# A two-layer transformer on one core: rows turned four tiles at a time, stores of the gating between weight loads, semaphores cleared by GpSimd

## The reference

```python
# layer 0 (layer 1 has another attention and no gating)
sh_a, sc_a, g_a, sh_m, sc_m, g_m = split(silu(c) @ w_mod[l] + b_mod[l])   # and the same for c_ctx
h  = x   * (1 + sc_a)  + sh_a          # "modulated" rows, the input of every projection
hc = ctx * (1 + csc_a) + csh_a
# mixer_ab: window attention on 512 columns, gating on the other 512
u, gv = gelu(h @ w_in[:, 768:1280]), gelu(h @ w_in[:, 1280:])
vn    = layer_norm(gv)                                  # (chunks of 128 tokens, 8 groups, 64)
b_out = u * (einsum('gpq,bnqgc->bnpgc', w_s, vn) + b_s)
y     = concat([a_out, b_out], -1) @ w_out              # and the same for ctx
x     = layer_norm(ALPHA * x + g_a * y)
x     = layer_norm(ALPHA * x + g_m * (relu(modulate(x) @ w1) ** 2 @ w2))
```

## Time and profile before

| | us |
|---|---|
| median of three executions | 2984.6 |
| the profiled execution | 2985.59 |
| its span, first to last instruction | 2983.8 |
| modulation stage | 0 to 29.4 |
| rows stage (0, kind 0) | 29.4 to 61.7 |
| window stage | 61.7 to 461.6 |
| gating stage | 461.6 to 506.6 |
| block 0 | 506.6 to 1537.1 |
| second rows stage | 1537.1 to 1589.4 |
| attention stage | 1589.4 to 2147.5 |
| block 1 | 2147.5 to 2983.8 |

### The profile page before, as it was taken

One profiled execution on the slowest core, in us unless ns is written; L12 is line 12 of the kernel. 1 busy time (PEld: TensorE's weight loads), 2 busy tenths in 40 slices (PEclk: granted clock), 3 DMA queues, 4 the chain that ended last, 5 costly groups with the idle time before them and its releaser, 6 DMA issues. The chain is left out here.

```text
span 2983.8 us, 40578 instructions
## 1 busy us (share of the span) xinstructions
PE 2799.8 (94%) x15614; PEld 2296.1 (77%) x15614; DVE 1361.5 (46%) x2159; ACT 912.1 (31%) x1704; POOL 533.6 (18%) x365
## 2 busy tenths in 40 slices
PE   6999995999999999999957999999799999999998
PEld 3666774788888888888846888888677888888886
DVE  3575454563333333333383555555555333333336
ACT  4244553341121121111224344443433212211222
POOL 0000000341121121121140000000034223323321
PEclk7999997999999999999978999999999999999999
DMA  6574225441011010010042111110256111111112
GB/s 251 184 307 157 70 67 186 147 136 43 28 48 36 28 56 28 28 56 28 30 146 83 36 36 51 36 36 8 85 141 191 48 45 48 56 42 42 56 42 57
DMA packets 192673, 238.95 MB, mean 80 GB/s; under 512 B 15992, under 2 KB 153840, under 8 KB 186416
## 3 DMA queue, kind: packets, MB, share of 16 engines
q1 hardware_dynamic: 192272, 237.30, 24.8%
q10 hardware_dynamic: 288, 0.10, 0.0%
HBM read 203.72 MB, written 37.88 MB: 81 GB/s over the span
## 5 line engine op out<-in xcount | busy, mean ns | idle before, releaser
L2173 DVE TENSOR_TENSOR y<-y,pair 128x1024 f32<-128x1024 f32 x280 | 341.5, 1220 | 334.9 <-PE pair L2307 334.9
L2305 PE MATMUL pair<-m_wbh,m_ath 128*128 128x512 f32 x1120 | 437.1, 390 | 4.2 <-DVE y L2173 2.9
L2307 PE MATMUL pair<-m_wbh,m_atl 128*128 128x512 f32 x1120 | 437.9, 391 | 0.0
L2306 PE MATMUL pair<-m_wbl,m_ath 128*128 128x512 f32 x1120 | 436.9, 390 | 0.0
L2227 DVE TENSOR_TENSOR m_atl<-m_sq,m_ath 128x512 fp32r<-128x512 f32 x156 | 100.8, 648 | 646.2 <-POOL m_sq L2078 646.2
L2032 ACT ACTIVATE m_rel<-pair 128x512 f32<-128x512 f32 x160 | 88.9, 555 | 983.6 <-PE pair L2331 973.1
L2078 POOL TENSOR_TENSOR m_sq<-m_rel 128x512 f32<-128x512 f32 x160 | 155.2, 970 | 1125.6 <-ACT m_rel L2032 1125.5
L2331 PE MATMUL pair<-hth,m0n_wal 128*128 128x512 f32 (+1 forms) x768 | 272.2, 354 | 0.0
L2330 PE MATMUL pair<-htl,m0n_wah 128*128 128x512 f32 (+1 forms) x768 | 272.1, 354 | 0.0
L2329 PE MATMUL pair<-hth,m0n_wah 128*128 128x512 f32 (+1 forms) x768 | 271.5, 354 | 0.0
L2305 PEld LDWEIGHTS pair<-m_wbh,m_ath 128*128 128x128 f32 x1120 | 210.3, 188 | 50.3 <-DVE y L2173 4.6
(11 more groups left out here) (270 smaller groups left out, 5239.8 us busy)
## 6 DMA issues: line engine op xcount, KB each, us to landing
a_ring<-in_w_mod SPq DMA_DIRECT2D x40, 1024.0 KB, 9.1
m_rawb<-in_mlp_w SPq DMA_DIRECT2D x64, 512.0 KB, 4.4
m_rawa<-in_mlp_w SPq DMA_DIRECT2D x60, 512.0 KB, 4.1
x_rows<-r_res SPq DMA_DIRECT2D x28, 512.0 KB, 5.0
r_raw<-cat_cols SPq DMA_DIRECT2D x18, 512.0 KB, 6.3
mod_w<-in_w_mod SPq DMA_DIRECT2D x8, 1024.0 KB, 12.3
r_xin<-in_x SPq DMA_DIRECT2D x16, 512.0 KB, 4.3
gate_pre<-a0g_gout SPq DMA_DIRECT2D x20, 256.0 KB, 2.0
```

The source lines that it names most:

```text
L2173: dve.tensor_tensor(k.y[:, t, :], k.y[:, t, :], k.pair[t % 2][:, :], ALU.add).then_inc(s_y, 1)
L2305: pe.matmul(o, ath[:, m, ts], bh[:, m, cols], start=m == 0, stop=False)
L2306: pe.matmul(o, ath[:, m, ts], bl[:, m, cols], start=False, stop=False)
L2307: i = pe.matmul(o, atl[:, m, ts], bh[:, m, cols], start=False, stop=m == M - 1)
```

## The change

It has three parts.

The first replaces `stage_rows(0, 0)` by a new `stage_first`. All ten row tiles are loaded ahead by the modulation stage, each with a semaphore of its own. The tokens are taken in groups of 512, 512 and 256. In a group TensorE turns block kt of all its tiles next to each other into bank kt, so that one ScalarE instruction applies scale and shift to 512 (or 256) columns. There are 24 such steps of one kt and one group. The copy to `hth` is made by VectorE in the even steps and by ScalarE in the odd ones; VectorE subtracts in all. `modt` has four places.

The second part is in the gating: the loads of `ab_w_out` are issued one behind each of the first eight stores, and `bot` has six places, so that `leave(t)` waits for the store of tile t-6.

The third part hands `clear_last` to GpSimd in every stage (at the attention and the window stage behind GpSimd's first memsets).

```diff
@@ Kept
-    def clear_last(self, dve):
+    def clear_last(self, pool):
         for s in self.dead:
-            dve.sem_clear(s)
+            pool.sem_clear(s)
@@ stage_modulation
-    x_ahead = nc.alloc_sbuf_tensor_at("r00_xin", [P, 3, D], F32, offset=k.after_ht)
-    s_ahead = [k.early(f"r00_x{i}") for i in range(3)]
+    x_ahead = nc.alloc_sbuf_tensor_at("r00_xin", [P, XT + CT, D], F32, offset=k.after_ht)
+    s_ahead = [k.early(f"r00_x{t}") for t in range(XT + CT)]
...
-            for t in range(3):
-                sp.dma_start(x_ahead[:, t, :], io["x"][0][t * P:(t + 1) * P, :]).then_inc(s_ahead[t], 16)
+            for t in range(XT + CT):
+                x = (io["x"][0] if t < XT else io["ctx"][0])[t % XT * P:(t % XT + 1) * P, :]
+                sp.dma_start(x_ahead[:, t, :], x).then_inc(s_ahead[t], 16)
@@ new
+def stage_first(nc, io, k):
+    sb = Place(nc, "r00", k.after_ht)
+    xin, s_x = k.ahead["x"]
+    sb.at += (XT + CT) * D * 4
+    NB = 4
+    modt = sb("modt", [P, NB, 512])
+    assert sb.at <= k.window_head
+    head = Place(nc, "a0h", k.window_head)
+    ahead = {}
+    for x in "kv":
+        ahead[x] = head(f"raw{x}", [P, KT, P]), k.early(f"a0_raw_{x}")
+        head.at += 2 * KT * P * 4
+    k.ahead["kv"] = ahead
+    sem = lambda n: k.sem(f"r00_{n}")
+    s_tr, s_mod, s_ha, s_hd, s_hl = [sem(x) for x in ("tr", "mod", "ha", "hd", "hl")]
+    groups = groups_of(TOK)
+    steps = [(a, n, kt) for a, n in groups for kt in range(KT)]
+    by_act = lambda i: i % 2 == 1
+    with nc.Block() as block:
+        @block.sync
+        def _(sp):
+            for i, x in enumerate("kv"):
+                sp.dma_start(ahead[x][0][:, :, :], io["ab_w_in"][0].rearrange("(k p) n -> p k n", p=P)[:, :, 512 + i * P:512 + (i + 1) * P]).then_inc(ahead[x][1], 16)
+        @block.gpsimd
+        def _(pool):
+            k.clear_last(pool)
+        @block.scalar
+        def _(act):
+            def high(i):
+                a, n, kt = steps[i]
+                act.wait_ge(s_mod, i + 1)
+                act.activation(k.hth[:, kt, a:a + n], modt[:, i % NB, 0:n], ACT.Copy).then_inc(s_ha, 1)
+            for i, (a, n, kt) in enumerate(steps):
+                col = lambda part: k.mod[:, 0, part * KT + kt, a // SEQ:a // SEQ + 1]
+                act.wait_ge(s_tr, i + 1)
+                if i >= NB:
+                    act.wait_ge(s_hl, i - NB + 1)
+                act.activation(modt[:, i % NB, 0:n], k.bank[kt][:, 0:n], ACT.Identity, scale=col(SC_A), bias=col(SH_A)).then_inc(s_mod, 1)
+                if by_act(i):
+                    high(i)
+        @block.vector
+        def _(dve):
+            for i, (a, n, kt) in enumerate(steps):
+                hi, v = k.hth[:, kt, a:a + n], modt[:, i % NB, 0:n]
+                dve.wait_ge(s_mod, i + 1)
+                if by_act(i):
+                    dve.wait_ge(s_ha, i // 2 + 1)
+                else:
+                    dve.tensor_copy(hi, v).then_inc(s_hd, 1)
+                    dve.wait_ge(s_hd, i // 2 + 1)
+                dve.tensor_tensor(k.htl[:, kt, a:a + n], v, f32(hi), ALU.subtract).then_inc(s_hl, 1)
+        @block.tensor
+        def _(pe):
+            for g, (a, n) in enumerate(groups):
+                tiles = range(a // P, (a + n) // P)
+                def turn(t, kt):
+                    pe.wait_ge(s_x[t], 16)
+                    if g:
+                        pe.wait_ge(s_mod, KT * (g - 1) + kt + 1)
+                    at = (t - tiles[0]) * P
+                    i = pe.transpose(k.bank[kt][:, at:at + P], xin[:, t, kt * P:(kt + 1) * P], k.ident[:, :])
+                    if t == tiles[-1]:
+                        i.then_inc(s_tr, 1)
+                if g == 0:
+                    for t in tiles:
+                        for kt in range(KT):
+                            turn(t, kt)
+                else:
+                    for kt in range(KT):
+                        for t in tiles:
+                            turn(t, kt)
@@ stage_mix
     gv, uu = [sb(x, [P, T, 512]) for x in ("gv", "uu")]
     bo = sb("bo", [P, 2, 512])
     wst, bst = sb("wst", [P, 8, P]), sb("bst", [P, 8])
-    bot = sb("bot", [P, 2, 4, P])
+    NT = 6
+    bot = sb("bot", [P, NT, 4, P])
     rstd, wsum, plus = sb("rstd", [P, 2, T]), sb("wsum", [P, 8]), sb("plus", [P, 512])
     assert sb.at <= k.mix_mv
     sem = lambda n: k.sem(f"gate_{n}")
@@ -1261,7 +1347,7 @@
     assert sb.at <= k.after_ht + 22 * D * 4
     s_wst, s_wsc, s_std, s_rec, s_sum, s_plus, s_norm, s_mix, s_bo, s_bt, s_bc = [sem(x) for x in (
         "wst", "wsc", "std", "rec", "sum", "plus", "norm", "mix", "bo", "bt", "bc")]
-    s_st = [sem("st0"), sem("st1")]
+    s_st = [sem(f"st{i}") for i in range(NT)]
     s_vt, s_ut = [sem(f"v{t}") for t in range(T)], [sem(f"u{t}") for t in range(T)]
     B = 3
     by_group = lambda x: x.unsqueeze(2).broadcast_to([P, 8, 64])
@@ -1272,13 +1358,17 @@
                 for x, s, part in ((gv, s_vt, 0), (uu, s_ut, 1)):
                     for i in (t, t + 1):
                         sp.dma_start(x[:, i, :], k.gpre_dram[part, i * P:(i + 1) * P, :]).then_inc(s[i], 16)
-            for u in range(KT):
-                sp.dma_start(raww[:, u, :], io["ab_w_out"][0][u * P:(u + 1) * P, :]).then_inc(s_raww[u], 16)
             for t in range(T):
                 sp.wait_ge(s_bc, t + 1)
-                sp.dma_start(k.cat_dram.rearrange("(j p) t -> p j t", p=P)[:, 4:8, t * P:(t + 1) * P], bot[:, t % 2, :, :]).then_inc(s_st[t % 2], 16)
-            for i in range(2):
-                sp.wait_ge(s_st[i], 16 * (T // 2))
+                sp.dma_start(k.cat_dram.rearrange("(j p) t -> p j t", p=P)[:, 4:8, t * P:(t + 1) * P], bot[:, t % NT, :, :]).then_inc(s_st[t % NT], 16)
+                if t < KT:
+                    sp.dma_start(raww[:, t, :], io["ab_w_out"][0][t * P:(t + 1) * P, :]).then_inc(s_raww[t], 16)
+            for i in range(NT):
+                sp.wait_ge(s_st[i], 16 * len(range(i, T, NT)))
+        @block.gpsimd
+        def _(pool):
+            k.clear_last(pool)
         @block.scalar
         def _(act):
@@ -1288,9 +1378,9 @@
             def leave(t):
                 act.wait_ge(s_bt, t + 1)
-                if t >= 2:
-                    act.wait_ge(s_st[t % 2], 16 * (t // 2))
-                act.activation(bot[:, t % 2, :, :], k.bank[6 + t % 2][:, :].rearrange("p (j q) -> p j q", q=P), ACT.Copy).then_inc(s_bc, 1)
+                if t >= NT:
+                    act.wait_ge(s_st[t % NT], 16 * (t // NT))
+                act.activation(bot[:, t % NT, :, :], k.bank[6 + t % 2][:, :].rearrange("p (j q) -> p j q", q=P), ACT.Copy).then_inc(s_bc, 1)
             act.activation(rstd[:, 0, :], mv[:, :, 1], ACT.Sqrt, bias=k.eps[:, 0:1]).then_inc(s_std, 1)
             act.wait_ge(s_rec, 1)
@@ -1303,7 +1393,6 @@
         @block.vector
         def _(dve):
-            k.clear_last(dve)
             dve.wait_ge(s_std, 1)
             dve.reciprocal(rstd[:, 1, :], rstd[:, 0, :]).then_inc(s_rec, 1)
             dve.wait_ge(s_wst, 1)
@@ build
-    stages = [(stage_modulation, ()), (stage_rows, (0, 0)), (stage_window, ()), (stage_mix, ()), (stage_block, (0,)),
+    stages = [(stage_modulation, ()), (stage_first, ()), (stage_window, ()), (stage_mix, ()), (stage_block, (0,)),
...
```

## The result

| | before | after |
|---|---|---|
| median of the runs side by side, us | 2985.7 | 2970.1 (2967.05 to 2971.86) |
| ratio, 95% interval | | 0.9948 (0.993 to 0.9965) |
| span of the profiled execution | 2983.8 | 2969.7 |
| first rows stage (now `stage_first`) | 32.3 | 27.9 |
| window stage | 399.8 | 397.1 |

Faster by 15.6 us, where the forecast took 13.0 off and came to 2971.6. The stages are taken from the first transfer that SP issues in each. Their sum says where the 14.1 us between the two spans lie: 4.3 in the first stage (5.2 forecast), 9.4 in the gating (7.8), 2.7 in the window stage (nothing forecast), less 2.3 in the others, which are each at most 1.0 longer.

What follows compares the result with a forecast made beforehand. The prediction took ScalarE's 80 narrow instructions to bound the first rows stage and the queue, with a store wait, the gating. Gains of 5.2 + 7.8 + 0 = 13.0 us gave 2971.6 us, own range 2966 to 2976.

Steps and rivals of the forecast that it cites:

- The first stage: First rows stage: wide ScalarE steps replace 80 narrow ones, ending at 56.4 us against 61.6; gain 5.2 us, bounds 1.5 to 8.7.
- The pair of steps: First rows stage: an even and an odd step on 512 columns, 0.67 + 0.67 + 0.62 + 0.05 = 2.0 us.
- The gating: Gating stage: the queue never runs dry and ends the stage at 498.9 in place of 506.7; gain 7.8 us.
- The 0.92 of a store: Gating queue: each store priced at 0.92 us, from 284 GB/s at a full share; 9.2 us for ten.
- rival A: Gating: loads and stores overlap in both directions, gain 16.3 us there, run 2963.1 us; chance 10%.
- Six places: Gating: six places in `bot` suffice, as store 0 lands near 479.6 and `leave(6)` comes near 482.
- The clears: All stages: moving the clears to GpSimd gains 0, since VectorE's saving is hidden; bounds 0 and 1.4 us.
- The wait that follows: End of the gating: the remaining wait is SP's for the last stores, about 8 us.
- B: First rows stage: wide steps gain nothing, a pair takes 2.5 us in place of 2.0, run 2976.8 us; chance 10%.
- C: Gating: the queue is fed unevenly, so half of the 7.8 us is gained, run 2975.5 us; chance 6%.
- D: Gating: SP becomes the bound at 3.79 us per store issue, stage 9.7 us later, run 2989.1 us; chance 3%.
- a later stage that differs by more than 2 us: Stages after the gains: a sign of a wrong forecast; they were to stay as before within 1 us each.

Runs made afterwards that it cites:

- e10_again: The kernel after, unchanged, measured once more beside other kernels: 2971.1 us, ratio 0.9946 against the kernel before.
- e11_places4: The kernel after with four places in `bot` in place of six: 2971.2 us, ratio 0.9948 against the kernel before.
- e13_dveclears: The kernel after with the clears back on VectorE in every stage: 2972.1 us, ratio 0.9951 against the kernel before.
- e6_blockwise: The kernel after with group 0 of the first stage turned block by block, not tile by tile: 2969.5 us, ratio 0.9938 against the kernel before.
- e5_places: The kernel before with six places in `bot` and nothing else, weight loads still ahead of all stores: 2981.2 us, ratio 0.9974.
- e7_late4: The block-by-block kernel with weight blocks 4 to 7 of `ab_w_out` loaded by block 0, not the gating: 2963.7 us, ratio 0.9922 against the kernel before.

## Why the prediction held, step by step

- **The first stage: right in kind, 0.9 too much.** The pair of steps is 2.0 us, as summed, though the wide instruction lasts 0.765 (estimated at 0.67, bound 0.75): the second of two starts 0.66 after the first (1.43 for both, less 0.765), and it is the distance that counts. What was mis-sized is the start: 34.4 forecast, 35.30 measured, 0.1 past my bound of 35.2. I let the clock rise after 16 transposes, as in the earlier trace rows; here all 25 before the first wide step ran at the low level, 0.21 us apart. It was this execution's clock: in e10_again, e11_places4 and e13_dveclears, with the same order of transposes, it rose after 14 to 18 of them, and the stage was 26.8 to 27.2 us, which is what I had forecast (27.0). e6_blockwise showed that the wait was for the order of the transposes.
- **The gating: mechanism right, the store's price too high.** 17.0 for the loads was right (16.9), and so was 10.5 for the weights, within 0.3 (8 x 1.28 is 10.2 in e5_places). The ten stores cost 7.6 us and not 9.2: loads landed at 471.65, the last store at 489.79, and 18.1 less 10.5 is 7.6. The 0.92 of a store came from the earlier trace rows, a window with two stores alone, scaled to a share of 1. But stores that were queued up behind each other moved 346 GB/s at a share of 1.12, 0.76 each, with no load among them (e5_places). So the 1.6 us are no piece of rival A: stores are cheaper than I took them to be, and not because they overlap with loads. The Trainium skill, "DMA: Bandwidth & Descriptors", section "Two DMAs through the same engine are not ordered", says that the read and write sides of an engine are separate queues. No gain from that is to be seen here: 1.99 us a pair mixed, 2.04 apart.
- **Six places: sufficient, and two more than needed.** Four do as well, and even the order alone brings 6.5 of the 9.4 in the stage.
- **The clears: nothing, as forecast**, alone (1.0003) and within the kernel after (0.9951 against 0.9946). The cover is the one named: idle matmuls in the window stage, the queue in the gating.
- **The wait that follows** is SP's for the last stores, 6.4 us where I had 8.
- **The rivals.** B: the wide instruction is 0.765 and so over the mark of 0.75 that I had set, but the pair is 2.0, and it is the pair that decides. C: the share was 1.03 from 469 to 489. D: no issue took over 1.53 us; the 3.8 of the earlier trace rows did not come back in the kernel after. In e5_places, with weights ahead, three stores' issues took 3.1, 5.1 and 4.2 us; the longest fell into the stretch from 480 to 487, in which the share was 1.03.
- **What I had not counted:** 2.7 us of the window stage, put at nothing. I had written that a later stage that differs by more than 2 us would make the prediction wrong. By that sentence it failed in one stage. That the total came out near is in part luck: 2.7 of the window stage and 1.6 of the gating too little, 0.9 of the first stage too much and 2.3 given back in block 0, attention and block 1 leave 1.1 us between the spans. By the medians the gain is 15.6 and not 13.0; the forecast of 2971.6 is only 1.5 off because it started from 2984.6, and the kernel before came to 2985.7 beside the kernel after.

## What to carry to other kernels

When a wait on a finished transfer holds an engine, look at what stands in the queue ahead of that transfer: more places and another order are two ways to the same gain, and neither can give more than the queue's work, which only a move to a stage with room in its queue takes away. Before a burst of wide instructions that need several tiles, turn the operands in the order in which they are used, block by block, so that the first one waits for the last load and not for all of the transposes. A stage that the edit doesn't touch can shift by 3 to 4 us between executions, with the granted clock, so take the gain of an edit from its own stage and use several executions for the rest.

## What the runs showed of the hardware

- On one queue, loads of 512 KB with 4 KB pieces went at 411 GB/s with a share of 1.03, and stores of 512-byte pieces at 346 GB/s with a share of 1.12 (e5_places, 480 to 487 and 489 to 491). The two alternating took 1.99 us a pair (kernel after), where the separate rates make 2.04.
- A share of 1 was not the ceiling for stores: scaling 253 GB/s at 0.89 up to a share of 1 gave 284, and 346 were reached.
- ScalarE's scale-and-bias out of PSUM took 0.765 us for 512 columns and 0.551 for 256, but a second one started 0.66 us after the first.
- The same program after the same 1.17 us of idle TensorE ran at 1.2 GHz in one execution and at 2.4 in another (e6_blockwise and e7_late4, the same up to that point).
